# A layer step in which the eight sample rows are multiplied with a quarter of the columns in each column group, in place of four partial sums and a summing product

## The reference

```
cols = split(u @ w_in)            # 4992 columns: HGRN2, differential and dilated heads
mix  = [hgrn2(...), diff_attention(...), dilated_attention(...)]
h = h + mix @ w_out               # 1024 x 1024
h = h + moe(rmsnorm(h))           # 16 experts, top 2 of one group of 4
gate = sigmoid(rmsnorm(h) @ ple_w_gate)
y = rmsnorm(h + gate * (p @ ple_w_proj))
```

## Time and profile before

| | |
|---|---|
| median of three timed runs | 1079.28 us |
| the profiled execution | 1074.52 us |
| its span, first to last instruction | 1072.8 us |
| mean granted TensorE clock | 0.937 |
| TensorE busy | 952.5 us (89%) |
| VectorE busy | 380.9 us (36%) |
| ScalarE busy | 240.0 us (22%) |
| GpSimd busy | 82.4 us (8%) |

### The profile page before, as it was taken

The page is one execution under the profiler, slowest core; times in us unless marked ns, Lnnn a source line. Parts: engine busy times, 40 slices in busy tenths (PEclk is TensorE's granted clock), DMA queues, the critical chain, the costliest instruction groups (busy, mean ns, idle before and its releaser), DMA issues.

```text
span 1072.8 us, 14361 instructions
## 1 busy us (share of the span) xinstructions
PE 952.5 (89%) x5739; PEld 482.2 (45%) x5739; DVE 380.9 (36%) x803; ACT 240.0 (22%) x573; POOL 82.4 (8%) x96
## 2 busy tenths in 40 slices
PE   3998999999999899988888998799999997993995
PEld 3444445554446567555445444343333342331442
DVE  3207445454212656535454124311111111112354
ACT  3116222220223233253222212101000000001335
POOL 1000000000001455000000000100000000002100
PEclk9998999996999999986798999799999998995998
DMA  6554233033136664253523605279999999996101
GB/s 206 193 199 177 30 137 138 1 137 141 30 137 222 226 180 141 69 187 94 178 99 113 257 21 238 96 272 353 381 387 406 399 409 395 398 403 209 42 20 61
DMA packets 72094, 208.67 MB, mean 195 GB/s; under 512 B 15937, under 2 KB 48148, under 8 KB 67548
## 3 DMA queue, kind: packets, MB, share of 16 engines
q1 hardware_dynamic: 57344, 184.73, 46.6%
q0 software_dynamic: 3936, 14.22, 3.9%
q10 hardware_dynamic: 10748, 8.80, 2.5%
HBM read 188.31 MB, written 38.25 MB: 211 GB/s over the span
## 4 chain that ended last, share of the span: by engine, by line
PE 72%; DMA 10%; DVE 9%; ACT 4%; SPq 2%; issue 2%; POOL 1%; ACTq 0%; DVEq 0%; POOLq 0%
PE ps L1939 16%; PE ps L2371 9%; PE ps L1944 7%; DMA EXPERT<-in_moe_w_up 6%; PE ps L2478 5%; PE ps L2256 5%; PE ps L2406 4%; PE ps L2380 3%; PE ps L1975 2%; PE ps L2326 2%; PE ps L1947 2%; PE ps L2021 1%; PE ps L2102 1%; PE ps L2048 1%; DMA EXPERT<-in_cache_win 1%
## 5 line engine op out<-in xcount | busy, mean ns | idle before, releaser
L1939 PE MATMUL ps<-xT,EXPERT 128*128 128x512 f32 x384 | 183.8, 622 | 1.2 <-DVE EXPERT L1278 1.2
L2371 PE MATMUL ps<-EXPERT,aF 128*32 128x512 f32 x1024 | 116.8, 609 | 19.2 <-DMA EXPERT<-in_moe_w_up 10.6
L1944 PE MATMUL ps<-EXPERT,xT 128*128 128x384 f32 (+1 forms) x384 | 118.7, 451 | 0.0
L1939 PEld LDWEIGHTS ps<-xT,EXPERT 128*128 128x128 f32 x384 | 71.3, 197 | 81.2 <-issue 78.4
L1944 PEld LDWEIGHTS ps<-EXPERT,xT 128*128 128x128 f32 x384 | 77.7, 236 | 25.5 <-issue 3.6
L2371 PEld LDWEIGHTS ps<-EXPERT,aF 128*32 128x32 f32 x1024 | 34.2, 112 | 97.6 <-issue 81.1
L2406 PE MATMUL ps<-EXPERT,dF 128*32 128x512 f32 x512 | 59.9, 610 | 3.3 <-ACT dF L1187 3.3
L2478 PE MATMUL ps<-EXPERT 128*128 128x512 f32 x128 | 57.4, 608 | 5.3 <-DVE EXPERT L1900 5.3
L1852 DVE TENSOR_TENSOR dF<-dF,ps 64x512 f32<-64x512 f32 x16 | 11.0, 690 | 136.8 <-ACT dF L1183 136.8
L2256 PE MATMUL ps<-EXPERT,xT 128*128 128x512 f32 x128 | 57.2, 598 | 1.1 <-ACT xT L1098 1.1
L1183 ACT ACTIVATE dF<-ps 64x512 f32<-64x512 f32 x16 | 9.4, 590 | 205.6 <-PE ps L2371 205.6
(11 more groups left out here) (444 smaller groups left out, 1226.3 us busy)
## 6 DMA issues: line engine op xcount, KB each, us to landing
EXPERT<-in_moe_w_gate SPq DMA_DIRECT2D x16, 2048.0 KB, 15.6
EXPERT<-in_moe_w_up SPq DMA_DIRECT2D x16, 2048.0 KB, 20.6
EXPERT<-in_moe_w_down SPq DMA_DIRECT2D x16, 2048.0 KB, 20.8
EXPERT<-in_w_in SPq DMA_DIRECT2D x13, 1536.0 KB, 6.5
out_win_sample<-in_cache_win SPq DMA_DIRECT2D x16, 1022.0 KB
aF<-in_cache_k_diff SPq DMA_DIRECT2D x32, 192.0 KB, 2.4
aF<-in_cache_v_diff SPq DMA_DIRECT2D x32, 192.0 KB, 2.5
Yd<-wk ACTq DMA_DIRECT2D x34, 128.0 KB, 9.1
```

Source lines behind the costliest of these rows:

```text
L1939: last = t.matmul(ps[:, u % 2, :], W_[:, c, c0:c0 + w], xT[:, c, 0:SEQ], start=(c == 0), stop=(c == DC - 1))
L1944: last = t.matmul(ps[:, u % 2, 0:w], rows_, W_[:, c, c0:c0 + w], start=(c == 0), stop=(c == DC - 1))
L2371: last = t.matmul(ps[32 * q:32 * q + 32, 2, :], xgT[:, c, 32 * (q % 2):32 * (q % 2) + 32], w[:, c, :], start=(c == 0), stop=(c == DC - 1))
```

## The change

The SM unit now runs every chunk on all four groups: group `q` multiplies with columns `96 q` to `96 q + 95` of the slab and accumulates over all eight chunks. The SS units, the buffers `part`, the second copy and `sel4`'s products are gone. ScalarE copies each group's 8 rows into its quarter of `samp`. `sample_product` does the same with quarters of 256 columns in one bank; VectorE adds the four quarters to the residual, and the last gate takes four sigmoids.

```diff
@@ projection_units, unit_marks, schedule
-    out = []
-    for n, un in enumerate(units):
-        out.append(un)
-        if n and units[n - 1][0] == "SM":
-            out.append(("SS", units[n - 1][1], 0, SLAB, None))
-    if out[-1][0] == "SM":
-        out.append(("SS", out[-1][1], 0, SLAB, None))
-    return out
+    return units
-    summed = {units[u][1]: u for u in range(len(units)) if units[u][0] == "SS"}
+    summed = {units[u][1]: u for u in range(len(units)) if units[u][0] == "SM"}
@@ order of the counts that the residual waits for
-        WO_AT = {(0, 0): 1, (0, 1): 2, (1, 0): 3, (1, 1): 4, (2, 0): 5, (NT, 0): 6, (2, 1): 7, (3, 0): 8, (3, 1): 9}
+        WO_AT = {(0, 0): 1, (0, 1): 2, (1, 0): 3, (1, 1): 4, (2, 0): 6, (NT, 0): 5, (2, 1): 7, (3, 0): 8, (3, 1): 9}
@@ SyncE, q_out
-                sp.wait_ge(S_["unit_pe"], PART0_LAST + 1)
@@ ScalarE, proj
                 if kind == "SM":
-                    if sl in LATER:
-                        act.wait_ge(S_["lev_pe"], NT * (LEVELS + 1))
-                    src, dst = src[:, 0:SLAB], part[sl in LATER]
-                elif kind == "SS":
-                    src, dst = src[0:NS, 0:SLAB], samp[:, sl * SLAB:(sl + 1) * SLAB]
+                    for q in range(4):
+                        at_ = sl * SLAB + q * QSL
+                        last = s.activation(samp[:, at_:at_ + QSL], src[32 * q:32 * q + NS, 0:QSL], ACT.Copy)
+                    last.then_inc(S_["unit_ok"], 1)
+                    return
@@ ScalarE, last gate
+                if i == NT:
+                    for q in range(4):
+                        last = s.activation(sig[0][0:NS, q * 256:(q + 1) * 256], ps[32 * q:32 * q + NS, 4, 0:256], ACT.Sigmoid)
+                    last.then_inc(S_["pg_sig"], 1)
+                    return
-            sample_parts(4, 2)
@@ VectorE, residual
+                if h is None:
+                    for q in range(4):
+                        own = slice(q * 256, (q + 1) * 256)
+                        last = v.tensor_tensor(XM[0:NS, i, own], XM[0:NS, i, own], ps[32 * q:32 * q + NS, bk, 0:256], ALU.add)
+                    last.then_inc(S_["hres_ok"], 1)
+                    return
@@ TensorE, proj
                     elif kind == "SM":
-                        last = t.matmul(ps[32 * (c % 4):32 * (c % 4) + 32, u % 2, 0:w], xS[:, c, :],
-                                        W_[:, c, :], start=(c < 4), stop=(c >= 4))
-                if kind == "SS":
-                    last = t.matmul(ps[0:NS, u % 2, 0:w], sel4, part[sl in LATER], start=True, stop=True)
+                        for q in range(4):
+                            last = t.matmul(ps[32 * q:32 * q + 32, u % 2, 0:QSL], xS[:, c, :],
+                                            W_[:, c, q * QSL:(q + 1) * QSL], start=(c == 0), stop=(c == DC - 1))
@@ TensorE, sample_product
-                for hf in range(2):
-                    for c in range(DC):
-                        last = t.matmul(ps[32 * (c % 4):32 * (c % 4) + 32, bank + hf, :], cols[:, c, 0:32],
-                                        w[c][:, hf * 512:(hf + 1) * 512], start=(c < 4), stop=(c >= 4))
-                last.then_inc(S_["sp_pe"], 1)
+                for c in range(DC):
+                    for q in range(4):
+                        last = t.matmul(ps[32 * q:32 * q + 32, bank, 0:256], cols[:, c, 0:32],
+                                        w[c][:, q * 256:(q + 1) * 256], start=(c == 0), stop=(c == DC - 1))
-            def sample_sum(bank, count):
-                pe.wait_ge(S_["sp_cp"], count)
-                for hf in range(2):
-                    last = t.matmul(ps[0:NS, bank + hf, :], sel4, PT[:, hf, :], start=True, stop=True)
-            sample_sum(2, 1).then_inc(S_["wo_pe"], 1)
```

More of the change, by code:

```diff
@@ L100, in projection_units @@
         units[-1], units[-2] = units[-2], units[-1]
-    out = []
-    for n, un in enumerate(units):
-        out.append(un)
-        if n and units[n - 1][0] == "SM":
-            out.append(("SS", units[n - 1][1], 0, SLAB, None))
-    if out[-1][0] == "SM":
-        out.append(("SS", out[-1][1], 0, SLAB, None))
-    return out
+    return units
 def unit_marks(units):
-    last = {sl: max(u for u in range(len(units)) if units[u][1] == sl and units[u][0] != "SS") for sl in range(NSLAB)}
-    summed = {units[u][1]: u for u in range(len(units)) if units[u][0] == "SS"}
+    last = {sl: max(u for u in range(len(units)) if units[u][1] == sl) for sl in range(NSLAB)}
+    summed = {units[u][1]: u for u in range(len(units)) if units[u][0] == "SM"}
     return last, summed
@@ L132, in schedule @@
     last, summed = unit_marks(units)
-    steps, todo = [], [(u, c, c + PART) for u, un in enumerate(units) for c in ((0,) if un[0] == "SS" else range(0, DC, PART))]
+    steps, todo = [], [(u, c, c + PART) for u in range(len(units)) for c in range(0, DC, PART)]
     def project_one():
@@ L372, in hybrid_kernel @@
         stK = work2.rearrange("p (b c v) -> p b c v", b=NS, c=3)
-        part = [kdil[0].rearrange("p g n -> p (g n)")[:, 0:SLAB], work[:, 2 * SEQ:2 * SEQ + SLAB]]
         kpage = [aF_[:, k * PAGES * SLAB:(k + 1) * PAGES * SLAB].rearrange("p (j n) -> p j n", j=PAGES)
@@ L535, in hybrid_kernel @@
         STEPS = schedule(UNITS)
-        H_END = STEPS.index(("state_out",))
-        LATER = {UNITS[st[1]][1] for st in STEPS[H_END:] if st[0] == "proj" and UNITS[st[1]][0] == "SM" and st[2] == 0}
-        PART0_LAST = max(SUMU[sl] for sl in range(NSLAB) if sl not in LATER)
+        QSL = SLAB // 4
         CU = dilated_units()
@@ L900, in proj @@
                 kind, sl, c0, w, at = UNITS[u]
-                if k1 < DC and kind != "SS":
+                if k1 < DC:
                     return
@@ L1117, in inv_rms @@
                 s.activation(rstd[0:r, i:i + 1], ssq[0:r, i:i + 1], ACT.Exp, scale=-0.5).then_inc(S_[sem_name], 1)
-            def sample_parts(bank, count):
-                act.wait_ge(S_["sp_pe"], count)
-                s.activation(PTf, ps[:, bank:bank + 2, :].rearrange("p b n -> p (b n)"),
-                             ACT.Copy).then_inc(S_["sp_cp"], 1)
             def half_columns(p):
@@ L1686, in residual @@
                 dve.wait_ge(S_["wo_pe"], WO_AT[i, h or 0])
-                both = slice(0, D) if h is None else slice(h * 512, (h + 1) * 512)
-                src = ps[0:r, bk:bk + 2, :].rearrange("p b n -> p (b n)") if h is None else ps[0:r, bk + h, :]
+                if h is None:
[4 more added lines that the diff above has]
+                    return
+                both = slice(h * 512, (h + 1) * 512)
+                src = ps[0:r, bk + h, :]
                 ins = v.tensor_tensor(XM[0:r, i, both], XM[0:r, i, both], src, ALU.add)
@@ L1934, in proj @@
                 if k0 == 0 and u >= 2:
-                    pe.wait_ge(S_["unit_ok"], u if kind == "SS" and UNITS[u - 1][0] == "SM" else u - 1)
+                    pe.wait_ge(S_["unit_ok"], u - 1)
                 for c in range(k0, k1):
@@ L2289, in _ @@
             pe.wait_ge(S_["hres_ok"], 1)
-            sample_product(xS, wout_, 2)
+            sample_product(xS, wout_, 2).then_inc(S_["wo_pe"], 1)
             columns_of(1)
@@ L2473, in ple @@
                 if i == NT:
-                    sample_product(hnT[0], [ple_[:, c] for c in range(DC)], 4)
-                    return sample_sum(4, 2).then_inc(S_["pg_pe"], 1)
+                    return sample_product(hnT[0], [ple_[:, c] for c in range(DC)], 4).then_inc(S_["pg_pe"], 1)
                 for hf in range(2):
```

6 lines of the change are left out of this document (2 added, 4 removed).

## The result

The changed kernel takes 1064.9 us (median of 4, 1061.8 to 1066.3) against 1080.2 us (median of 4, 1078.3 to 1083.5) of the kernel before in the same runs: ratio 0.985, 95% interval 0.981 to 0.989. A second measurement of the same two kernels gave 1058.7 against 1076.7 us, ratio 0.982 (0.977 to 0.987). So it is faster by 1.5 to 1.8%, and the forecast of 1062 was 3 us off. Medians here are over all runs of a kernel, ratios and intervals over its fast runs (none more than 1.5% above its fastest). The two profiled executions differ by less than the medians do, 1065.5 against 1074.5 us. The two second traces are from different chips.

What follows compares the result with a forecast made beforehand. TensorE was taken as full among the heads, waiting between levels at short pieces, and behind a ScalarE-VectorE chain at their start. 3 + 3 - 18.5 - 2 - 2.7 = -17.2 us gave 1062, range 1056 to 1067, chance 0.60.

Steps and rivals of the forecast that it cites:

- The price of a sample unit: Projection sample units: 21 ns a pass, so 1.33 us contiguous, 0.45 for a single piece, 0.79 for a pair.
- first rival: Pass price decides, in contiguous units, heads and half the levels' pieces: at 54 ns a pass +21 us, 1083; chance 0.06.
- A: Up to the start of the levels: 5.3 us lost by later sigmoids, 2.3 us won, so +3 us.
- third rival: Start costs more: idle keeps clock low into levels, copies cost 2 us, a pass 27 ns; 1070, chance 0.22.
- B: Levels and state part, 101.55 to 275 us: 7.1 - 3.6 - 1.5 + 1 = +3 us.
- the four pieces of a full unit: Levels and state: four pieces of a following full unit come in as four summing units leave, costing 7.1 us.
- C: Heads, 275 to 467 us: less TensorE work and no wait at the first query, together -18.5 us.
- the stall: Heads, first sample query: TensorE's 3.06 us wait goes because SyncE issues the query's DMA earlier, -3.1 us.
- second rival: Heads' gain doesn't arrive: VectorE, GpSimd and cache loads end last once TensorE is thinner; 1074, chance 0.12.
- The slab: Heads: weight slab now behind the query's stores and loads, some 20 us, covered by about 40 us of TensorE work; nothing counted.
- D: w_out's sample product: the 1.81 us sum goes and the product is slightly shorter, -2 us.
- E: The tail: product -0.2, no copy and no sum -2.9, four sigmoids instead of one +0.4; -2.7 us.

Runs made afterwards that it cites:

- act_back: Changed kernel with ScalarE's sigmoids behind one unit of slab 2 and logarithms behind three, instead of two and four; 1053.1 us, ratio 0.975 to the kernel before.
- one_copy: Changed kernel with one 8x384 copy after each sample unit in place of four of 8x96, sample columns partly wrong; 1062.1 us, ratio 0.985 to the kernel before.
- order_kept: Changed kernel with every step at its place before the change (laid out with summing units counted, then taken out); 1055.7 us, ratio 0.979 to the kernel before.
- twice: Changed kernel with every sample product of the projections issued two times and halved in the copy; 1068.3 us, ratio 0.991 to the kernel before.
- short_mult: Changed kernel with GpSimd's first product for each cached query cut to a quarter, page scores incomplete; 1054.0 us, ratio 0.979 to the kernel before.

## Why the prediction was right, point by point

**The price of a sample unit: right.** 1.46 us contiguous (1.33 plus the 0.12 for the change of shape that I left out there), 0.47 for a single piece (0.45), 0.80 for a pair (0.79), 20.6 ns a pass (21). The first rival, 54 ns a pass, is out: neither a start price nor the weight loads bound these passes. The 60 cycles a matmul of the Trainium skill's "TensorEngine Tiling (Array Packing)", Instruction Overhead, would by estimate be 25 ns a pass at 2.4 GHz, and the sequencer price in its "TensorE: Matmul & The Clock Gate", Back-to-back issue gap, is about 62 ns with hardware decode off; the trace shows neither, at 20.6.

**A, +3: right.** Measured +3.2 in the first traces and +2.9 between the second ones. The idle 7.94 us before the level, with the 1.60 us ahead of them, were said to be some 9. act_back shows the two parts. The third rival, that this wait would keep the clock low into the levels, didn't come: the stretch at 1.2 GHz is 6.8 us long as before, and as the levels start later, more of it falls into the wait (3.3 us of it lie in the levels instead of 5.6).

**B, +3: wrong, -2.7** (173.5 and 174.0 us before, 170.8 and 171.2 after). Three terms make up the difference. The granted clock had no term in the sum: it is low for 2.2 us less in the levels (2.6 in the second traces) and for 13.7 us instead of 17.1 in the state part, and at half the speed that is 1.1 and 1.7 us. The copies were nothing instead of 1 us (one_copy). And the 7.1 us for the four pieces of a full unit were counted in full, beside a mere -1.5 for the sample pieces. These get shorter by 2.6 us at their own prices (8 single pieces and 4 pairs before, 4 and 6 now). By themselves they would have left waits, as I said, but the incoming pieces filled them: TensorE is idle for 4.5 us of the levels before, 6.7 in order_kept and 3.9 after. My own account of what bounds the kernel said that TensorE waits between levels whenever the piece there is short, and I used this only for the shorter sample pieces. The fourth piece stood in the state part, where the clock rose from 0.68 to 0.74 and hid it. Why that stretch of low clock is shorter stays open.

**C, -18.5: the terms for TensorE's work are right, the one for the stall is not.** Measured -12.2 (191.7 to 179.5) in the first traces and -15.6 (191.6 to 176.0) in the second. The work terms add up to -15.4, and in the second traces, with 3.4 us at the low clock, TensorE is busy for 14.7 us less. But its idle time in this part falls only from 5.3 to 4.8 us (5.2 to 4.2), where the stall's -3.1 was counted. Without the new wait the sum is met: -18.8 with GpSimd's product short, and -19.2 in twice, whose 180.5 us hold 8.0 us of added passes and a wait of 0.54 us. The stall at the first query went, as said, but my reading of it was incomplete, and its cause came back elsewhere. I had put the 3.06 us down to the query's DMA. VectorE's timeline of before and GpSimd's beside it show what else stood there:
```profile
350.44 2.92 DVE L1453 TENSOR_SCALAR wk<-wk,small 128x256 f32<-128x256 f32 x1
353.40 1.37 DVE L1454 SCALAR_TENSOR_TENSOR wk<-wk,small 128x256 f32<-128x256 f32 x1
```
```profile
349.79 3.42 POOL L813 TENSOR_TENSOR aF<-aF,EXPERT 128x1536 f32<-128x1536 f32 x1 [2.40 <-DMA EXPERT<-q_d]
```
The first of the two operations ahead of that wait took 2.92 us instead of 0.35, beside a GpSimd product, and the second 1.37 instead of 0.48. That is 3.5 us more than alone, and so by estimate the whole of the 3.06 us. The change moved the query products against the heads' steps, and another one now meets VectorE's normalisation of a head. With it came a wait of 1.7 to 2.3 us. In the heads there are also 3.4 to 10.2 us at 1.2 GHz that before had not. Together they are 3.1 to 6.6 us, against short_mult, about 2.2 of them the wait. A part of the second rival (VectorE and GpSimd end last once TensorE is thinner) thus came true, by a way that it didn't name: not the sum of VectorE's work, but the length of one operation. The slab that I had counted as covered made nothing wait.

**B and C together.** Predicted -15.5, measured -14.9 and -18.4. The forecast came out because the errors nearly cancel: B came out 5.7 us better than said and C 2.9 to 6.3 worse; this part of it was luck.

**D, -2, and E, -2.7: right.** The product takes 3.59 us and the sum's 1.81 are gone: -1.8. The tail is 2.4 us shorter; the four sigmoids took 0.53 us more than the one, not 0.4, and the product 3.71, not 3.5.

**The block behind the heads** does not move rigidly. I had assumed this from w_out on and had no term for the part ahead of it. From the dilated scores to w_out it takes 112.7 and 119.7 us before, 115.1 and 112.0 after; from w_out to the end 493.3 and 497.0 before, 493.3 and 490.5 after. This is the spread that separates the traces' difference (9.5 us in the first pair, 29.6 in the second) from that of the medians (15 to 18).

## What to carry to other kernels

When a step leaves and another moves into its place, ask at each of the two places whether TensorE is full or waits there: the same piece costs its whole length among full steps and much less between two waits. When TensorE gets thinner, look at what each engine runs beside the others, and not only at how busy it is: a VectorE operation that lands beside a long one of GpSimd can take several times as long (here 2.90 us for 0.42), and whether that costs anything depends on how much work TensorE has behind it. And where splitting a small product over columns instead of over its sum gets rid of a second product, the gain is the second product's; the narrow passes came at the price of their columns.

## What the runs showed of the hardware

- A VectorE operation of 128x384 that takes 0.42 us took 2.90 and 2.27 us beside a GpSimd product of 128x1536 (3.43 us), and one of 128x256 took 2.44 us in place of 0.35 (2.92 in the trace of before). With the GpSimd product at 128x384 (1.00 us, over before it starts) it took 0.63, beside the next product. Each of them ends 0.1 to 0.25 us after GpSimd's operation does. An operation with two inputs, L1439, took 1.50 us in place of 0.62, and 3.53 in place of 0.48. VectorE's reductions beside it aren't stretched (128x1536 takes 1.74 us beside GpSimd and 1.75 without). "SBUF — State Buffer" in the Trainium skill, Who interferes with whom, says that the two engines share one pair of SBUF ports, that the operation which comes first keeps it to its end while the other stands still, and that a tensor_scalar or an operation with two SBUF inputs can be subject to this while a reduction on this chip never is. The traces agree in all three, for the order in which GpSimd's operation comes first. Had I held this rule against the order of VectorE's steps, the rival of a moved collision would have had a place and a price.
- Passes of 96 columns on four column groups follow each other at 20.6 ns at 2.4 GHz, which is the price of their columns, 20 ns by the earlier trace rows, and nothing on top. Each piece takes 0.14 us beyond its passes, whether it has 64, 32 or 16 (1.46, 0.80 and 0.47 us). That this is the change of shape between this piece and the products around it, whose weights have 128 columns, fits, but no run separates it from other costs of a piece.
- The granted clock fell to 1.2 GHz for 3.4 to 6.8 us with the waits at 371 (2.30 and 1.66 us) and at 342 in order_kept (5.04), but not with those of 1.78 and 2.25 us in act_back, nor with the 3.06 us at the first query before the change. What tells them apart is open. For this kernel the spread goes with the clock: in nearly every set of runs the slower ones have the lower mean granted clock (the four of the first measurement are the exception), and two runs of the changed kernel on one chip took 1052.9 us at a mean granted clock of 0.945 and 1061.1 us at 0.931.
